# Channel norms of a two-layer encoder trunk: square root and reciprocal in place of logarithm and exponential, with shorter warm runs and one adaLN sum moved

## What is computed

```python
def rmsnorm(x, g, eps=EPS):
    y = x32 * lax.rsqrt(jnp.mean(x32 * x32, axis=-1, keepdims=True) + eps) * g
def layernorm(x, g, b, eps=EPS):
    mu = jnp.mean(x32, axis=-1, keepdims=True)
    var = jnp.mean(jnp.square(x32 - mu), axis=-1, keepdims=True)
    y = (x32 - mu) * lax.rsqrt(var + eps) * g + b
...
    for layer in range(DEPTH):                       # 2
        mod = c_act @ ada_w[layer] + ada_b[layer]
        sh1, sc1, g1, sh2, sc2, g2 = jnp.split(mod, 6, axis=-1)
        h = rmsnorm(x, norm_g[layer, 0]) * (1.0 + sc1[:, None]) + sh1[:, None]
        y = diff_attention(...)  if kind == 0 else conformer_conv(...)
        x = x + g1[:, None] * y
        h = rmsnorm(x, norm_g[layer, 1]) * (1.0 + sc2[:, None]) + sh2[:, None]
        x = x + g2[:, None] * conv_ffn(h, ff_w_up[layer], ff_w_dw[layer], ff_b_dw[layer], ff_w_down[layer])
    return rmsnorm(x, final_g)
```

## Time and profile before

| | us |
|---|---|
| median of 3 runs | 1266.55 |
| lowest, highest | 1265.33, 1268.99 |
| the profiled execution | 1264.87 |
| its span, first to last instruction | 1263.1 |
| PE busy in it | 1231.2 (97%) |
| DVE, ACT, POOL busy | 706.3, 564.0, 531.3 |

### The profile page before, as it was taken

The page is one execution under the profiler, slowest core; times in us unless marked ns, Lnnn a source line. Parts: engine busy times, 40 slices in busy tenths (PEclk is TensorE's granted clock), DMA queues, the critical chain, the costliest instruction groups (busy, mean ns, idle before and its releaser), DMA issues.

```text
span 1263.1 us, 16845 instructions
## 1 busy us (share of the span) xinstructions
PE 1231.2 (97%) x5504; PEld 983.2 (78%) x5504; DVE 706.3 (56%) x1160; ACT 564.0 (45%) x896; POOL 531.3 (42%) x265
## 2 busy tenths in 40 slices
PE   8999999989999999999999999999999999999996
PEld 6877777667888888888888777577888888888884
DVE  5677767753766633346887899972533333340002
ACT  4356566644544334442224665662544444442221
POOL 2333322123443344454442688644344444454440
PEclk7899999999999999999998999999999999999998
DMA  9744443222455532236773222113233332232321
GB/s 360 234 136 146 149 166 116 101 100 67 160 184 189 166 100 99 88 105 226 243 242 100 96 68 67 33 34 100 67 100 100 100 100 91 91 107 93 106 77 66
DMA packets 45639, 157.04 MB, mean 124 GB/s; under 512 B 5536, under 2 KB 5792, under 8 KB 45600
## 3 DMA queue, kind: packets, MB, share of 16 engines
q1 hardware_dynamic: 44928, 156.21, 36.9%
q10 hardware_dynamic: 672, 0.34, 0.1%
HBM read 154.10 MB, written 2.42 MB: 124 GB/s over the span
## 4 chain that ended last, share of the span: by engine, by line
PE 83%; DVE 10%; issue 2%; ACT 2%; DMA 1%; SPq 0%; DVEq 0%; ACTq 0%
PE psum L917 25%; PE psum L918 24%; PE psum L919 24%; DVE psum L1754 3%; PE psum L1245 2%; PE psum L947 2%; PE psum L928 1%; DMA ada_first<-ada_w 1%; DVE psum L1480 1%; DVE pt_lo L1489 1%; PE psum L1074 1%; DVE acc L1331 1%; DVE psum L1355 1%; PE psum L1270 1%; PE psum L1101 1%
## 5 line engine op out<-in xcount | busy, mean ns | idle before, releaser
L502 POOL TENSOR_TENSOR w_lo<-w_raw,w_hi 128x1024 fp32r<-128x1024 f32 (+1 forms) x192 | 456.1, 2391 | 677.1 <-ACT w_hi L589 677.1
L917 PE MATMUL psum<-h_hi,w_hi 128*128 128x512 f32 x1152 | 465.9, 404 | 4.3 <-DVE x L1584 2.2
L919 PE MATMUL psum<-h_hi,w_lo 128*128 128x512 f32 x1152 | 452.0, 392 | 0.0
L918 PE MATMUL psum<-h_lo,w_hi 128*128 128x512 f32 x1152 | 451.8, 392 | 0.0
L917 PEld LDWEIGHTS psum<-h_hi,w_hi 128*128 128x128 f32 x1152 | 219.0, 190 | 54.6 <-issue 7.6
L919 PEld LDWEIGHTS psum<-h_hi,w_lo 128*128 128x128 f32 x1152 | 218.2, 189 | 46.9
L918 PEld LDWEIGHTS psum<-h_lo,w_hi 128*128 128x128 f32 x1152 | 218.9, 190 | 45.5 <-issue 3.4
L589 ACT ACTIVATE w_hi<-w_raw 128x1024 fp32r<-128x1024 f32 (+1 forms) x192 | 195.8, 1032 | 84.7 <-DMA w_raw<-w_tiles 84.6
L917 PE MATMUL psum<-a_hi,w_hi 128*128 128x512 f32 x352 | 137.1, 389 | 0.9 <-issue 0.9
L919 PE MATMUL psum<-a_hi,w_lo 128*128 128x512 f32 x352 | 137.0, 389 | 0.0
L918 PE MATMUL psum<-a_lo,w_hi 128*128 128x512 f32 x352 | 137.0, 389 | 0.0
(11 more groups left out here) (185 smaller groups left out, 1331.6 us busy)
## 6 DMA issues: line engine op xcount, KB each, us to landing
w_raw<-w_tiles SPq DMA_DIRECT2D x160, 512.0 KB, 3.3
ada_buf<-ada_w SPq DMA_DIRECT2D x32, 512.0 KB, 3.3
w_raw<-w_tiles SPq DMA_DIRECT2D x32, 448.0 KB, 3.1
ada_late<-ada_w SPq DMA_DIRECT2D x28, 512.0 KB, 5.3
ada_mid<-ada_w SPq DMA_DIRECT2D x20, 512.0 KB, 4.6
ada_first<-ada_w SPq DMA_DIRECT2D x16, 512.0 KB, 10.0
x<-x_in SPq DMA_DIRECT2D x4, 512.0 KB, 7.0
bias<-rel_scratch SPq DMA_DIRECT2D x8, 256.0 KB, 6.5
```

What stands on the lines that cost most here:

```text
L502: nc.gpsimd.tensor_tensor(w_lo[:, slot, 0:k], w_raw[:, (ph.tile + l) % 2, 0:k], f(w_hi[:, slot, 0:k]), ALU.subtract).then_inc(lo_done, 1)
L917: nc.tensor.matmul(dst, w_hi[:, slot, k], rhs_hi, start=first, stop=False)
L918: nc.tensor.matmul(dst, w_hi[:, slot, k], rhs_lo, start=False, stop=False)
L919: return nc.tensor.matmul(dst, w_lo[:, slot, k], rhs_hi, start=False, stop=last)
```

## The change

All five channel norms and the layer norm take ScalarE's Sqrt and then VectorE's reciprocal, in place of Ln and Exp. No table load stands between the two steps, the copy of delta to PSUM goes, and so do the semaphores of both. The table that is loaded ahead of each norm is the Sqrt one; at norm 0 an Exp table load and a one-column activation follow the root. The reciprocal is in VectorE's program right ahead of the first scaled tile. The warm runs go from 18 to 12 at norms 1 and 3 and from 24 to 13 at the layer norm. In the layer norm VectorE subtracts delta (now from SBUF) from one tile and GpSimd from seven. The seventh late chunk gets a home of its own (acc_last, in the place of pad_g), its product on TensorE stands behind the layer norm's sums, and VectorE's bias for it (late_out, second part) in the layer norm.

```diff
-        acc_late = at("acc_late", [P, LATE, S], F32, h_base + 4 * 2 * S * 4)
+        acc_late = at("acc_late", [P, LATE - 1, S], F32, h_base + 4 * 2 * S * 4)
+        acc_last = at("acc_last", [P, S], F32, offset_of["pad_g"])
...
-            for m in range(DK // 2, DK):
+            for m in range(1, DK):
                 nc.gpsimd.tensor_tensor(y[:, m], y[:, m], delta[:], ALU.subtract).then_inc(pool_mean, 1)
...
-            def inverse_rms(n):
+            def root_mean_square(n):
                 act.wait_ge(sq_added, DK * (n + 1))
-                nc.scalar.activation(rms[:], psum[:, OB], ACT.Ln, bias=sm(EPS6), scale=1.0 / D).then_inc(log_ready, 1)
-                act.wait_ge(log_ready, n + 1 if n < 3 else n + 2)
-                nc.scalar.activation(psum[:, OB], rms[:], ACT.Exp, scale=-0.5).then_inc(rms_ready, 1)
+                nc.scalar.activation(rms[:], psum[:, OB], ACT.Sqrt, bias=sm(EPS6), scale=1.0 / D).then_inc(root_ready, 1)
...
-            load_table(ACT.Ln)
-            act.wait_ge(delta_ready, 1)
-            nc.scalar.activation(psum[:, DELTA_AT], delta[:], ACT.Copy).then_inc(delta_copied, 1)
+            load_table(ACT.Sqrt)
             act.wait_ge(var_ready, 1)
-            nc.scalar.activation(rstd[:], rstd[:], ACT.Ln, bias=sm(EPS6)).then_inc(log_ready, 1)
-            act.wait_ge(log_ready, 4)
-            nc.scalar.activation(psum[:, RSTD_AT], rstd[:], ACT.Exp, scale=-0.5).then_inc(ln_rstd, 1)
+            nc.scalar.activation(rstd[:], rstd[:], ACT.Sqrt, bias=sm(EPS6)).then_inc(root_ready, 1)
             load_table(ACT.Silu)
...
             square_sum(1, 2)
-            keep_warm(18)
+            keep_warm(12)
...
-                ada_product(WARM, acc_late[:, q], at_=4 * q)
+                if q < LATE - 1:
+                    ada_product(WARM, acc_late[:, q], at_=4 * q)
+                else:
+                    ada_product(LAST_OUT, acc_last[:])
...
             last_ada(0)
             square_sum(2, 1)
-            for q in range(1, LATE):
+            for q in range(1, LATE - 1):
                 last_ada(q)
...
                 dev_sums(n)
-            keep_warm(24)
+            last_ada(LATE - 1)
+            keep_warm(13)
             pairs(PW2, 4 * DK, x_done, 2 * DK, 2)
             square_sum(3, 2)
-            keep_warm(18)
+            keep_warm(12)
...
+            def inverse(count):
+                dve.wait_ge(root_ready, count)
+                V.reciprocal(psum[:, OB], rms[:]).then_inc(dve_step, own.tick())
+                dve.wait_ge(dve_step, own.now())
...
             first_gain(0)
-            dve.wait_ge(rms_ready, 1)
+            inverse(1)
             norm_tiles(0, 0, DK // 2)
...
             norm(2)
-            late_out()
+            late_out(0, LATE - 1, psum[:, WARM, 0:4 * (LATE - 1)])
...
-            dve.wait_ge(delta_copied, 1)
-            for m in range(DK // 2):
-                V.tensor_tensor(y[:, m], y[:, m], psum[:, DELTA_AT], ALU.subtract).then_inc(dve_step, own.tick())
-            dve.wait_ge(ln_rstd, 1)
+            V.tensor_tensor(y[:, 0], y[:, 0], delta[:], ALU.subtract).then_inc(dve_step, own.tick())
+            late_out(LATE - 1, LATE, psum[:, LAST_OUT, 0:4])
+            dve.wait_ge(root_ready, 4)
+            V.reciprocal(psum[:, RSTD_AT], rstd[:]).then_inc(dve_step, own.tick())
             dve.wait_ge(dve_step, own.now())
             for m in range(DK + 1):
-                if m >= DK // 2:
-                    dve.wait_ge(pool_mean, min(m, DK - 1) - DK // 2 + 1)
+                if m:
+                    dve.wait_ge(pool_mean, min(m, DK - 1))
```

More of the change, by code:

```diff
@@ L256, in trunk @@
         SUM_AT, SQ_AT = 0, 1
-        DELTA_AT, RSTD_AT, SILU_AT = 4, 5, 6
+        LAST_OUT, RSTD_AT, SILU_AT = 4, 5, 6
         params_in, consts_in = sem("params_in"), sem("consts_in")
@@ L277, in trunk @@
         sq_ready = sem("sq_ready")
-        log_ready = sem("log_ready")
-        rms_ready = sem("rms_ready")
+        root_ready = sem("root_ready")
         h_hi_ready = sem("h_hi_ready")
@@ L288, in trunk @@
         diag_ready = sem("diag_ready")
-        delta_copied = sem("delta_copied")
-        devsq_ready, ln_rstd, ln_silu = sem("devsq_ready"), sem("ln_rstd"), sem("ln_silu")
+        devsq_ready, ln_silu = sem("devsq_ready"), sem("ln_silu")
         used = sem("used")
@@ L332, in piece @@
             return t[n] if isinstance(n, int) else t[bass.ds(n, 1)].rearrange("o p n -> p (o n)")
-        EPS5, NEG_LAM, SUB_G, EPS6, LSUM, LEXP, TABLE = 0, 1, 2, 3, 4, 6, 50
+        EPS5, NEG_LAM, SUB_G, EPS6, LSUM, LEXP, TABLE, TABLE_SQRT = 0, 1, 2, 3, 4, 6, 50, 51
         GATE_COL = 40
@@ L623, in _ @@
             act.wait_ge(dve_step, 2)
-            nc.scalar.activation(rms[:], psum[:, OB], ACT.Ln, bias=sm(EPS6), scale=1.0 / D).then_inc(log_ready, 1)
-            act.wait_ge(log_ready, 1)
-            nc.scalar.activation(psum[:, OB], rms[:], ACT.Exp, scale=-0.5).then_inc(rms_ready, 1)
+            nc.scalar.activation(rms[:], psum[:, OB], ACT.Sqrt, bias=sm(EPS6), scale=1.0 / D).then_inc(root_ready, 1)
+            load_table(ACT.Exp)
             split_tile(HEAD, 0, 1)
@@ L657, in norm_act @@
             def norm_act(n, then=None):
-                inverse_rms(n)
+                root_mean_square(n)
                 if n == 4:
@@ L1402, in norm_tiles @@
                     if m > lo:
-                        if n == 2 and m <= LATE:
+                        if n == 2 and m < LATE:
                             dve.wait_ge(ada_mm, LATE_CH + m)
@@ L1435, in norm @@
                     gain_of(n, 0, DK)
-                dve.wait_ge(rms_ready, n + 1)
+                inverse(n + 1 if n < 3 else n + 2)
                 if n < 4:
@@ L1606, in mid_out, with late_out @@
                 V.tensor_tensor(to, psum[:, 4, 0:4], ab, ALU.add).then_inc(sc_read, 1)
-            def late_out():
-                dve.wait_ge(ada_mm, LATE_CH + LATE)
-                first, b = 4 * LATE_CH, PARAMS["ada_b"] + 4 * LATE_CH
-                V.tensor_tensor(mod[:, first:first + 4 * LATE], psum[:, WARM, 0:4 * LATE], prm[:, b:b + 4 * LATE],
+            def late_out(lo, hi, sums):
+                dve.wait_ge(ada_mm, LATE_CH + hi)
+                first, b = 4 * LATE_CH + 4 * lo, PARAMS["ada_b"] + 4 * LATE_CH + 4 * lo
+                V.tensor_tensor(mod[:, first:first + 4 * (hi - lo)], sums, prm[:, b:b + 4 * (hi - lo)],
                                 ALU.add).then_inc(sc_read, 1)
-                dve.wait_ge(sc_read, LATE0 + MID + 1)
+                dve.wait_ge(sc_read, LATE0 + MID + (1 if hi < LATE else 2))
             def up(layer):
@@ L1681, in late_pieces @@
                         k = 2 * (q % 4) + kk
-                        ada_part(ada_late[:, q % 4, kk], k, tile_of(acc_late, lin(i, c, 2)),
+                        total = acc_last[:] if isinstance(i, int) else tile_of(acc_late, lin(i, c, 2))
+                        ada_part(ada_late[:, q % 4, kk], k, total,
                                  lin(i, 8 * (LATE_CH + c) + k, 16))
```

2 lines of the change are left out of this document (1 added, 1 removed).

## The result

The changed kernel takes 1280.66 us (median of 4 runs, 1275.84 to 1282.89) where the kernel before takes 1266.59 (4 runs, 1265.33 to 1268.99). The ratio is 1.0112, 95% interval 1.0089 to 1.0135: **slower by 1.1%**. The prediction was 1258.0, faster.

What follows compares the result with a forecast made beforehand. TensorE was taken as the bound, with 83% of the chain of waits. Gains of 3.7+2.8+1.4+1.1-0.4 = 8.6 us against the median of 1266.55 gave 1258.0 us, range 1254.5 to 1262.5.

Steps and rivals of the forecast that it cites:

- One pass an element gives the reciprocal 0.69 us: VectorE's 128x512 reciprocal in each norm, priced from its 128x2 row; taken as 0.69 us between bounds 0.69 and 4.5.
- The rival of eight passes: The reciprocal takes eight passes, costing 3.77 us more in each norm; 1279 us in all, chance 0.06.
- Norms 1 and 3: Earlier scaled tiles and warm runs of twelve passes start TensorE's wide products sooner; 1.85 us gained at each.
- The shorter warm runs let the clock fall: Rival at norms 1, 3 and the layer norm: each clock fall costs 1.5 us; 1262.5 us, chance 0.10.
- Norm 2: Wide products start earlier behind five chunks of small sums, with the clock expected to fall; 2.8 us gained, between 1.2 and 4.0.
- comes back 3 us after wide products resume as it did: At norm 2, after its fall the clock returns to 2.4 GHz 3 us after wide products restart, leaving 2.8 us gained.
- Layer norm: Without the table load and exponential, the first Silu starts earlier; 1.4 us gained, between 0.9 and 1.75.
- I see no fall from that: In the layer norm, the 13-pass warm run ends 1.2 us before TensorE starts, and the clock stays up.
- Norm 4: Nothing runs beside this norm, so the shorter path to VectorE's first scaled tile counts fully; 1.1 us gained.
- Norm 0: The reciprocal stands in VectorE's queue and delays the scaled tiles; 0.4 us lost, between 0 and 0.72.

Runs made afterwards that it cites:

- one_pass: The changed kernel with each wide reciprocal replaced by a one-pass minimum with 0.5 over the same tile, leaving out the inverse; 1259.44 us, ratio 0.9955.
- widths: The changed kernel with the reciprocal cut by columns: 256+256 at norm 2, 384+128 at norm 3, 64+448 at norm 4; 1279.95 us in one run.
- norm0_early: The changed kernel with norm 0's reciprocal moved ahead of the first adaLN output; 1278.49 us, ratio 1.0103.
- warm_cover: The changed kernel with warm runs of 20, 24 and 20 passes instead of 12, 13 and 12; 1275.76 us, ratio 1.0084.
- log_exp_warm: log_exp with 24 warm passes in the layer norm and two 128-column passes before each of norm 2's last four small sums; 1263.78 us, ratio 0.9991.
- log_exp: The changed kernel with logarithm, table load and exponential back in all norms, reciprocals removed, other edits kept; 1264.75 us, ratio 1.0004.
- norm0_log: The changed kernel with logarithm, table load and exponential put back in norm 0 alone; 1277.59 us, ratio 1.0083.
- one_table: log_exp with one activation table set holding both logarithm and exponential loaded ahead of each norm; 1259.84 us, ratio 0.9943.

## Why the prediction was wrong

- **The step that failed is "One pass an element gives the reciprocal 0.69 us", in the part on its price.** It measures 3.36 us, 2.67 more in each norm. The bounds of 0.69 to 4.5 us held it, but the range of the time was built on the lower end alone. The argument for that end was that the 128x2 row leaves 152 to 156 ns as its fixed part with one pass and 141 with eight, beside 153 for its neighbours. With what was measured it leaves 145. A difference of 8 ns between instructions of different kinds decided a slope that was then multiplied by 510: an error of 10 ns at two elements is 2.6 us at 512. The two rows could not tell the cases apart, and a chance of 0.06 for the slower one had nothing behind it. The Trainium skill (VectorE: DVE Perf Modes, First, the fixed hardware budget) says that the reciprocal iterates its divide with a repeat count of 8; the trace now shows 6.28 ns an element, the time of six passes of 1.05: many times one pass, though not eight times. Whether it is the iteration that takes the time, no run here shows.
- **The rival of eight passes** priced what came: it decides from 2.4 us, and its path terms for norms 1, 3 and 4 and the layer norm (3.77 us a norm) scale to 2.67. Its sum of 1279 us came near the 1280.7 by luck, since it left out the clock, 6.2 us, and charged 1.1 us more for each reciprocal. The stated range, which ended at 1262.5, left it out.
- **Norms 1 and 3.** The path was right apart from the price: one_pass gained 1.60 and 1.65 of the 1.85. "The shorter warm runs let the clock fall" (0.10) happened in the changed kernel, but as a consequence of the reciprocal: the run was cut for a path that then grew. In one_pass it did not happen at these two. A fall cost 1.6 us at norm 1 and 2.6 at norm 3, not 1.5 each; the size belongs to the execution, for in the profiles of widths and norm0_early norm 3 has eight slow products and the layer norm 13 and 14, and the stages from the layer norm to norm 4 take 428.2 to 428.5 us together in all three.
- **Norm 2.** The fall was foreseen. The step "comes back 3 us after wide products resume as it did" was wrong: in every kernel profiled here with one-column sums, it came back 6.8 us after it fell (10.2 in warm_cover and log_exp_warm), however early the wide products came: down from 686.2 to 693.0 before, from 686.7 to 693.5 in one_pass. So an earlier start only put more products at 1.2 GHz: 0.94 us gained with the assumed price, not 2.8, and under the lower bound of 1.2, which had let the clock out.
- **Layer norm.** "I see no fall from that" was wrong. 13 passes were too few even at the assumed price (seven slow products in one_pass, eight in log_exp, none with 24 in log_exp_warm): 0.2 us gained there, not 1.4. Part of that was a term of the sum: the passes were put at 0.33 us each, 4.3 together, and took 3.15, so TensorE stood idle for 2.30 us in one_pass and not 1.2. The sum for the path was right, 4.66 us from root to wide product against 6.23. VectorE's subtraction beside GpSimd ended 0.84 us after the root's start (841.66), for the 0.92 that was expected.
- **Norm 4.** 1.18 us in one_pass for the predicted 1.1; the changed kernel lost 1.47, as 2.67 more makes of it.
- **Norm 0.** Its place in VectorE's queue was the right reading. By norm0_log it cost 3.1 to 3.7 us, about the full length of the reciprocal, where the prediction had 0.4 of 0.72.
- **The moved chunk** was not tried alone. In log_exp, with the old exchange, the first wide product of norm 2 comes 1.7 us sooner after the logarithm (5.18 against 6.92), and the stage gains 0.8: the rest was lost to the clock.

The move of three subtractions to GpSimd was not tried alone either. In log_exp the layer norm's path from the logarithm on is as long as before (6.23 us in both), so no gain or harm of it can be seen there.

## What to carry over

A cost per element cannot be read from an instruction of two elements: divide the uncertainty of its fixed part by the elements, multiply by those you need, and let the range hold both ends. Read the granted clock behind every gap on TensorE, since a gap is paid twice, as a wait and then as longer products; a warm run should reach the moment at which its successor is ready (in warm_cover's layer norm a run that ended 1.06 us short of it let the clock fall), so it is to be re-fitted to the path as measured, after the path has changed. And before replacing functions to save a table load, see whether one table set holds both. Last, where the stretch ahead of the first changed place varies by microseconds, compare the stages behind it and not the medians alone.

## What was unexpected of the hardware

- VectorE's reciprocal costs 6.28 ns an element in fp32, and a cut into two instructions costs no more than the whole (3.37 us for 256+256 against 3.36).
- Products of one column did not hold TensorE's clock, although the profile counts the engine busy all through (3.00 of 3.00 us in the first window of the earlier trace rows), nor did they when mixed with 128-column passes (0.50 at 681 in log_exp_warm). The same sums with 64 or 128 columns did, at no loss: the first wide product came 4.18 us after the logarithm, and 6.08 in one_table with the one-column sums.
- After a fall in norm 2 the clock stayed down for 6.8 us, and in two runs for 10.2, although wide products had resumed meanwhile.
